# Chunk inverses of a bidirectional RWKV-7 recurrence: one matrix of the doubling kept in the other half of the partitions

## The reference

```python
    def step(s, inp):
        r_t, w_t, k_t, v_t, aa_t, bb_t = inp
        sa = jnp.einsum('dbhij,dbhj->dbhi', s, aa_t)
        s = s * w_t[..., None, :] + sa[..., :, None] * bb_t[..., None, :] + v_t[..., :, None] * k_t[..., None, :]
        y_t = jnp.einsum('dbhij,dbhj->dbhi', s, r_t)
        return s, y_t
```

## Time and profile before

| | us |
|---|---|
| median of 3 executions (3582.23 to 3590.2) | 3582.69 |
| span of the profiled execution, first to last instruction | 3583.4 |
| TensorE busy | 3214.0 (90%) |
| VectorE busy | 1414.6 (39%) |
| ScalarE busy | 984.3 (27%) |
| GpSimd busy | 161.1 (4%) |

### The profile page before, as it was taken

How to read it: one execution, slowest core, us unless ns; L and a number is a source line. 1 busy time by engine, 2 the same in 40 slices (tenths; PEclk the granted TensorE clock), 3 DMA queues, 4 the chain that set the end, 5 groups by cost and what they waited for, 6 DMA issues and landing times. The chain is left out here.

```text
span 3583.4 us, 63958 instructions
## 1 busy us (share of the span) xinstructions
PE 3214.0 (90%) x25849; PEld 2100.8 (59%) x25850; DVE 1414.6 (39%) x2400; ACT 984.3 (27%) x1768; POOL 161.1 (4%) x222
## 2 busy tenths in 40 slices
PE   3999889887699999999999979987899899878998
PEld 2888678676233333333333348865588688655786
DVE  5545645646311111111111157354623464546333
ACT  2333323312011111111111122343522323435321
POOL 0000000002200000000000100000000000000000
PEclk8999899888799999999999989997999999979999
DMA  6630330325799999999989843231032233310331
GB/s 225 227 121 20 102 100 6 102 76 223 282 409 374 409 379 351 409 369 354 408 342 383 316 164 84 76 49 36 14 117 94 64 90 94 49 36 1 106 94 59
DMA packets 273123, 646.39 MB, mean 180 GB/s; under 512 B 36890, under 2 KB 97050, under 8 KB 270978
## 3 DMA queue, kind: packets, MB, share of 16 engines
q1 hardware_dynamic: 251314, 604.07, 46.6%
q0 software_dynamic: 6224, 21.24, 1.6%
q10 hardware_dynamic: 15360, 17.85, 1.6%
HBM read 599.83 MB, written 43.27 MB: 179 GB/s over the span
## 5 line engine op out<-in xcount | busy, mean ns | idle before, releaser
L1746 PE MATMUL ps<-raw,ex_xT 128*64 128x512 f32 x3072 | 679.0, 594 | 3.6 <-DMA raw<-in_w_dram 3.6
L1746 PEld LDWEIGHTS ps<-raw,ex_xT 128*64 128x64 f32 x3072 | 218.7, 137 | 418.7 <-issue 409.2
L1845 DVE TENSOR_SCALAR ex_gl<-ps 128x256 f32<-128x256 f32 x96 | 40.7, 424 | 949.1 <-PE ps L1746 949.1
L1746 PE MATMUL ps<-raw,ex_aT 128*64 128x512 f32 x1536 | 349.1, 596 | 3.4 <-DMA raw<-in_w_dram 3.4
L1746 PEld LDWEIGHTS ps<-raw,ex_aT 128*64 128x64 f32 x1536 | 105.5, 137 | 214.9 <-issue 207.2
L2006 PE MATMUL ps<-zhi,hl 128*128 128x512 f32 (+1 forms) x448 | 169.7, 379 | 0.0
L2004 PE MATMUL ps<-zhi,hh 128*128 128x512 f32 (+1 forms) x448 | 169.1, 377 | 0.5 <-DVE hl L2134 0.5
L2005 PE MATMUL ps<-zlo,hh 128*128 128x512 f32 (+1 forms) x448 | 168.5, 376 | 0.0
L2551 PE MATMUL ps<-uu_hi,hh 128*128 128x512 f32 x384 | 151.3, 394 | 10.6 <-DVE uu_lo L2663 10.6
L2553 PE MATMUL ps<-uu_hi,hl 128*128 128x512 f32 x384 | 152.9, 398 | 0.0
L2552 PE MATMUL ps<-uu_lo,hh 128*128 128x512 f32 x384 | 152.2, 396 | 0.0
(11 more groups left out here) (574 smaller groups left out, 5961.2 us busy)
## 6 DMA issues: line engine op xcount, KB each, us to landing
raw<-in_w_dram SPq DMA_DIRECT2D x384, 1024.0 KB, 18.9
oT<-in_w_in_dram SPq DMA_DIRECT2D x64, 512.0 KB, 3.7
u_raw<-in_w_in_dram SPq DMA_DIRECT2D x24, 1024.0 KB, 5.2
expert_out<-xn SPq DMA_DIRECT2D x4, 4096.0 KB, 16.5
expert_out<-ex_yrow ACTq DMA_DIRECT2D x98, 128.0 KB, 5.6
late_ada<-in_w_ada_dram SPq DMA_DIRECT2D x12, 1024.0 KB
early_w<-in_w_in_dram SPq DMA_DIRECT2D x10, 1024.0 KB, 6.6
mT<-in_w_ada_dram SPq DMA_DIRECT2D x4, 2048.0 KB, 19.8
```

What stands on the lines that cost most here:

```text
L1746: mm = pe.matmul(o, x, M["raw"][:, (slot + LATE_SLOTS) % RING, k, h * 512:(h + 1) * 512], start=(s >= 8 and kk == 0), stop=(kk == 7))
```

## The change

The coupling matrix (section 2 of `m`) and the running inverse `x` of each chunk move to the other half of the partitions; `y`, `xt` and the other sections of `m` stay. So `score` and `score_context` write the `bt` part with the output half exchanged; `score`'s second 64 columns (those for r, section 3 of `m`) stay, so its `bt` part is split into two calls of 64 columns. `product_y` reads `m` and `x` in the other half and writes y to the chunk's own. In `product_x` the calls of the X and the T product alternate, unit by unit: two that cross (rows of one half, columns of the other), then two straight ones; `x_prod` is given at the X product's last pair, `t_prod` at the T product's. `nearest` writes its product with the halves exchanged into columns 0 to 255, and a second, transposed product without exchange into columns 256 to 511; VectorE starts `xt` from that one in place of the copy out of `m`. Nothing outside `rwkv_chunks` is changed.

```diff
@@ -800,12 +800,16 @@
                 for d in range(2):
                     for t2 in range(2):
                         tt = 2 * g + t2
-                        for sec, name in enumerate(("kt", "bt")):
+                        for h, c2 in quads(True):
+                            hs, cs = halves[h], halves[c2]
+                            both = W["ar"][hs, d, tt, :, CH * c2:CH * c2 + CH]
+                            pe.matmul(ps[cs, SCORE_BANK[g] + 2 * d + h, t2 * 256:t2 * 256 + P], W["kt"][hs, d, tokens(tt, c2)], both, start=True, stop=True)
+                        for part in range(2):
                             for h, c2 in quads(True):
-                                hs, cs = halves[h], halves[c2]
-                                both = W["ar"][hs, d, tt, :, CH * c2:CH * c2 + CH]
-                                mm = pe.matmul(ps[cs, SCORE_BANK[g] + 2 * d + h, t2 * 256 + sec * P:t2 * 256 + sec * P + P],
-                                               W[name][hs, d, tokens(tt, c2)], both, start=True, stop=True)
+                                hs, cs = halves[h], halves[c2 if part else 1 - c2]
+                                at = t2 * 256 + P + part * CH
+                                mm = pe.matmul(ps[cs, SCORE_BANK[g] + 2 * d + h, at:at + CH], W["bt"][hs, d, tokens(tt, c2)],
+                                               W["ar"][hs, d, tt, part, CH * c2:CH * c2 + CH], start=True, stop=True)
                     mm.then_inc(scores, 1)
 
             def score_context(g):
@@ -815,7 +819,7 @@
                         tt = 2 * g + t2
                         for sec, name in enumerate(("kt", "bt")):
                             for h, c2 in quads(True):
-                                hs, cs = halves[h], halves[c2]
+                                hs, cs = halves[h], halves[1 - c2 if sec else c2]
                                 at = d * 256 + t2 * P + sec * CH
                                 mm = pe.matmul(ps[cs, SCORE_BANK[g] + h, at:at + CH], W[name][hs, d, tokens(tt, c2)],
                                                W["ar"][hs, d, tt, 0, CH * c2:CH * c2 + CH], start=True, stop=True)
@@ -825,11 +829,15 @@
                 for d in range(2):
                     for t2 in range(2):
                         tt = 2 * g + t2
+                        at = (2 * d + t2) * CH
+                        for h, c2 in quads(True):
+                            hs, cs = halves[h], halves[1 - c2]
+                            pe.matmul(ps[cs, (Y_BANK, T_BANK)[h][g], at:at + CH], W["ar"][hs, d, tt, 0, CH * c2:CH * c2 + CH],
+                                      W["bt"][hs, d, tokens(tt, c2)], start=True, stop=True)
                         for h, c2 in quads(True):
                             hs, cs = halves[h], halves[c2]
-                            at = (2 * d + t2) * CH
-                            mm = pe.matmul(ps[cs, (Y_BANK, T_BANK)[h][g], at:at + CH], W["ar"][hs, d, tt, 0, CH * c2:CH * c2 + CH],
-                                           W["bt"][hs, d, tokens(tt, c2)], start=True, stop=True)
+                            mm = pe.matmul(ps[cs, (Y_BANK, T_BANK)[h][g], 256 + at:256 + at + CH], W["bt"][hs, d, tokens(tt, c2)],
+                                           W["ar"][hs, d, tt, 0, CH * c2:CH * c2 + CH], start=True, stop=True)
                 mm.then_inc(near, 1)
 
             def blocks(bank, at, lhs, rhs):
@@ -849,16 +857,29 @@
                     pe.wait_ge(started, g + 1)
                 else:
                     pe.wait_ge(x_out, n - nq + 1)
-                blocks(Y_BANK[g], col, lambda cs, u: m[g][cs, u, 2 * CH:3 * CH], lambda cs, u: x[g][cs, col(u):col(u) + CH]).then_inc(y_prod, 1)
+                for u in range(8):
+                    at = slice(col(u), col(u) + CH)
+                    for c2 in range(2):
+                        far = halves[1 - c2]
+                        mm = pe.matmul(ps[halves[c2], Y_BANK[g], at], m[g][far, u, 2 * CH:3 * CH], x[g][far, at], start=True, stop=True)
+                mm.then_inc(y_prod, 1)
 
             def product_x(n):
                 g, l = n % nq, n // nq
                 pe.wait_ge(y_out, n + 1)
                 if l:
                     pe.wait_ge(t_out, n - nq + 1)
-                if l < nl - 1:
-                    blocks(Y_BANK[g], col, lambda cs, u: xt[g][cs, col(u):col(u) + CH], lambda cs, u: y[g][cs, col(u):col(u) + CH]).then_inc(x_prod, 1)
-                blocks(T_BANK[g], col, lambda cs, u: y[g][cs, col(u):col(u) + CH], lambda cs, u: xt[g][cs, col(u):col(u) + CH]).then_inc(t_prod, 1)
+                for u in range(8):
+                    at = slice(col(u), col(u) + CH)
+                    if l < nl - 1:
+                        for c2 in range(2):
+                            cs = halves[c2]
+                            mx = pe.matmul(ps[halves[1 - c2], Y_BANK[g], at], xt[g][cs, at], y[g][cs, at], start=True, stop=True)
+                        if u == 7:
+                            mx.then_inc(x_prod, 1)
+                    for cs in halves:
+                        mt = pe.matmul(ps[cs, T_BANK[g], at], y[g][cs, at], xt[g][cs, at], start=True, stop=True)
+                mt.then_inc(t_prod, 1)
 
             def rows_of(u, g):
                 return 2 * g + u % 2, halves[u // 2 % 2]
@@ -1008,12 +1029,12 @@
                         dve.tensor_tensor(to, by_dir(ps[:, SCORE_BANK[g] + h, :]), strict, ALU.mult).then_inc(masked, 1)
                     dve.wait_ge(masked, 2 * LAT + 2)
                 dve.wait_ge(eyes, 2 * g + 2)
-                done(dve.copy_predicated(by_dir(xt[g]), table("turned1"), m[g].rearrange("p (d u) s -> p d u s", d=2)[:, :, :, 2 * CH:3 * CH]))
                 dve.wait_ge(near, g + 1)
-                pick = bc(S("near1").rearrange("p (d s) -> p d s", d=2), 2, 2).bitcast(U32)
+                pick, turned_pick = (bc(S(name).rearrange("p (d s) -> p d s", d=2), 2, 2).bitcast(U32) for name in ("near1", "turned1"))
                 for h in range(2):
-                    last = dve.copy_predicated(by_dir(x[g])[:, :, 2 * h:2 * h + 2, :], pick,
-                                               ps[:, (Y_BANK, T_BANK)[h][g], 0:256].rearrange("p (d t s) -> p d t s", d=2, t=2))
+                    bank = ps[:, (Y_BANK, T_BANK)[h][g], :].rearrange("p (a d t s) -> p a d t s", a=2, d=2, t=2)
+                    dve.copy_predicated(by_dir(x[g])[:, :, 2 * h:2 * h + 2, :], pick, bank[:, 0, :, :, :])
+                    last = dve.copy_predicated(by_dir(xt[g])[:, :, 2 * h:2 * h + 2, :], turned_pick, bank[:, 1, :, :, :])
                 last.then_inc(started, 1)
 
             def advance(n):
```

## The result

The changed kernel takes 3600.26 us (median of 5 runs, 3595.76 to 3601.75), the kernel before, on the same chip, 3582.69 (5 runs, 3581.41 to 3590.20): ratio 1.0045, 95% interval 1.0031 to 1.0058. So it is slower by 0.45%, some 16 us (17.6 between the two medians), where 3589 had been forecast. The profiled execution spans 3600.0 us against 3583.4: +16.6.

The account below looks back on a forecast made before the run. TensorE's array and its instruction supply (256 per 3.7 us) were taken to bound the loop 1% apart. Stages +3 us and slow clock +3 gave +6 on the median 3582.69, hence 3589 us; 8 in 10 within 3566 to 3602.

Parts of the forecast that it names:

- The bound: Chunk-stage loop: array at 14.6 ns an instruction, supply at 14.45 (256 per 3.7 us); the change lifts only the array's limit.
- Rival 1: Loop: instruction supply doesn't bind, packets 2.5 us apart; -9.4 us a stage, -38 in all, 3545 us; chance 12%.
- rival 4: Loop: idle 1.2 us per block takes TensorE's clock down to 1.2 GHz, 47 us more, 3636 us; chance 3%.
- The joint product: X and T products in the loop: 32 calls go from 1.87 us to 0.93, array time saved 11.2 us a stage.
- The openings: Chunk stages up to the first masked value product: 320 more instructions a stage, +15.0 us over the four.
- The walk: Step-by-step timing of the second stage's start with its block ends: value product at 18.4 us against 14.41, +4.0.
- the clock: Chunk stages: idle before the value product brings 1.2 GHz in three to four stages, about 1.0 us each, +3 us.
- The rests: Chunk stages from the value product on: the second's 56.0 us against 58.4, paced by blocks 3.7 us apart.
- rival 3: Chunk stages: slower supply, from 3.85 us a block; rests give nothing back, openings lose 15 to 18.4 us; 3597 to 3601; 25%.
- Nothing outside the four chunk stages should move: Sign for the rest of the kernel: no time change there; the added instructions make five blocks exactly.
- The likeliest case: Whole kernel: 3589 us, the same within the 0.3% (10.7 us) a measurement tells; chance of same 0.54.
- the case given 0.29: Whole kernel slower, over 3593.4 us: slower supply, clock drop in the loop, or the forecast's upper edge; chance 0.29.

Follow-up runs that it names:

- sequence version: Changed kernel with all 16 X calls, then all 16 T calls, instead of alternating; everything else as changed: 3603.64 us, ratio 1.0052.
- the added calls: Changed kernel with eight more straight calls beside each y product from the fifth step on, 352 instructions a stage more: 3616.64 us, ratio 1.0072.
- the waits: Changed kernel with extra, already satisfied semaphore waits on TensorE after each unit of the X and T products: 3640.28 us, ratio 1.0153.
- the best version: Kernel before with product_wu's two calls made one, and q with the first G product in one call: 3570.61 us, ratio 0.9949.

## Why the prediction was right or wrong

**The bound: right.** "Two limits, 1% apart, and the change lifts only one." The block of 256 instructions at 3.7 us, taken from twelve blocks of the tails, holds through the loop at 3.66 (49 blocks of the four stages in 179.3 us). Rival 1, the array's gain of 38 us, didn't come; the packets didn't move to 2.5 us. Nor did rival 4: the rests have a granted clock of 0.95 to 1.00. The alternation undone moves the stages by 1.2 us.

**The joint product: right.** In the loop it runs at the rate of `nearest`, four matmul records every 58 ns, which is 29 ns a call (38 of the product's 64 matmul records start between 320.00 and 320.54 us; the block ends there, and the rest come behind the stop). Two row halves in one PSUM bank cost nothing visible.

**The openings: right but for the fourth.** Worked out 18.4, 18.4, 18.7 and 17.1, measured 17.69, 18.06, 18.00 and 20.53. The walk had the block ends where they are: in the first stage, with the first end at 85, the stops come after 342, 598, 854 and 1110 records, the last in the middle of XT(0), and in the second at 7.5 and 14.7 us (7.4 and 14.8 foreseen). The value product of the first stage waits for 2.52 us behind VectorE (2.8 foreseen). The 4 us at 1.2 GHz at the head of the second and third openings cost nothing: the sequence version, with the same instructions at 2.4 GHz, takes 18.1 and 18.2 there. The fourth misses by 3.4 us, and it is tempting to put this down to the clock, for half of the 6.9 us at 1.2 GHz within it is 3.4. But the sequence version has the same opening with the same block ends, and went through it at 2.4 GHz:

```profile
707.35:726.57 19.22, 12.43 (x576) 11.66 (x576) 10.11 (x17) 1.19 (x2) 3.39 (x6) 1.00 0.02 4
```

So the clock's part is 1.3 us at most, and the other 2.1 were missing in the walk. Both kernels stop after 230 and 486 records; the second stop falls into the first `nearest` and lasts till 7.4 us, so VectorE's first copy stands behind 4.5 us of idle time (2.14 in the first stage). The working for this stage isn't given, so which of its steps was too short stays open.

**The rests: direction right, size short.** Worked out 224 us without the slow clock, measured 229.6. The worked one counts 3947 instructions behind the second opening where the rest has 3968 records beside its waits, which is worth half a microsecond a rest at most. They gave back 5.0 us, so rival 3, "give nothing back", is wrong as a mechanism, though its time, 3597 to 3601, is the one that came.

**The terms that were mis-sized: what the rests give back, and in part the clock.** Without the clock the openings were worked out at 72.6 us and the rests at 224.2, together +3, and the clock was to add 3 more. Measured were 74.3 and 229.6, +10.3. Seven stretches at 1.2 GHz with 31 us in the stages came in place of three or four of 3.4. In the openings the clock can explain 1.3 of the 1.7 us that are missing. Those of the sequence version, without it, add up to the 72.6 that were worked out, by luck: the fourth is 2.1 longer than the walk and the first three together 2.1 shorter. The rests gave back 5.0 us where 10.4 were worked out. Three of them hold 16 us at 1.2 GHz, whose price isn't separated; the fourth, without any, took 56.9 where 56.3 was worked out. The clock alone doesn't make the cost: between the two versions with wu in one call, with 10 and 14 us at 1.2 GHz in the stages, the change costs 9.4 us there, of which the clock's can be 1.7, and the rests give back 2.0 (223.1 and 221.1 us). Why they give back so little stays open.

**"Nothing outside the four chunk stages should move": wrong.** +6.1 us came from behind them, 8.5 at the router's products by the clock alone, the same instructions at 1.2 instead of 2.4 GHz. It isn't tied to the change as such. Two profiles go the other way; the kernel before with `nearest` twice:

```profile
885.23:903.73 18.50, 18.14 (x82) 17.56 (x81) 1.53 (x3) 3.40 (x5) 16.32 (x7) 0.50 1.01 399
```

and the changed kernel with wu in one call:

```profile
875.85:884.05 8.20, 8.20 (x71) 7.96 (x70) 2.65 (x3) 3.73 (x4) 5.21 (x3) 1.00 1.02 417
```

The first has its router products at 1.2 GHz, the second at 2.4. So it is throughout: five profiles have them at 2.4 GHz (before, before with wide `y`, before and changed with wu in one call, the added calls) and take 2810.2 to 2812.0 us after the last chunk stage; six have them at 1.2 GHz (the changed kernel, its sequence version, the waits, its wide `y`, `nearest` twice, wu and q in one call) and take 2814.9 to 2818.1. The two experiments whose numbers aren't the reference's are left out. What puts a kernel on one side stays open; for that stage only its start has moved, and a shift alone wasn't tried. So of the 17 us some 10 lie in the stages that were changed, and some 6 go with where the clock happened to be. This bears on the best version too: it has the slow router, so its 0.5% holds with the clock on the wrong side.

**The likeliest case** was "within 0.3%" (0.54), the measurement is 0.45% slower, inside the range of 3566 to 3602 but in the case given 0.29. The sum came out 11 us short: 4 within the stages, 6 in the clock behind them, and 1 between medians and profiled executions. Rival 3's time is the upper edge of the range, so a cost of this size was held possible, but by a mechanism of which only half came: the openings lost what it said, and the rests gave back something.

## What to carry to other kernels

Count a loop's instructions as well as its array time. A float32 call is four instructions, and TensorE got 256 of them in 3.66 us here, so a loop of 64x64 calls in two quarters (14.6 ns an instruction) already stands at that pace. Packing more quarters then saves array time that turns into stops marked "issue" 256 instructions apart, and every call added in front of the loop to make the packing possible is paid, here at 8 ns an instruction (6.3 us for the 768 of `nearest`) to 20 (10.2 us for the 512 of `score`). What paid was to merge two calls over the same stationary matrix into one with twice the columns: 11.6 us for 768 instructions. And before a difference is put down to the clock, look for a version with the same instructions whose clock was steady: half the slow time gave 3.4 us for an opening in which the clock can explain 1.3.

## What the runs showed of the hardware

- A satisfied wait that stands as an instruction of its own between TensorE's calls cost 50 ns (38.4 us for 768), more than three times an instruction's share of a block. Four such waits in a row became two instructions of their own.
- A float32 call over the full 128x128 array with 64 columns takes 0.24 us (8 in 2.00 us). A quarter call in a two-quarter run takes 58 ns, so one wide call costs four of these and does the work of two.
- The granted clock of a stage that nobody touched differs from one kernel to the next: the router's products took 10.0 us at 2.4 GHz or 18.5 at 1.2, and which it was went with no single edit (five profiles with the first, six with the second).
- Data steer the time: wrong numbers in the chunk stages cut the expert stage from 3072 to 2944 records, so the total of a kernel whose numbers aren't the reference's says little here; its stages do.
